# RWKV-7 recurrence on one core: value pieces in halves, three copies moved to ScalarE, and a new hand-written order of the four interleaved programs

## What is computed

```python
def _wkv_step(S, inp):
    r_t, w_t, k_t, v_t, a_t, b_t = inp
    Sa = jnp.einsum('bhvk,bhk->bhv', S, a_t)
    S = S * w_t[:, :, None, :] + Sa[..., None] * b_t[:, :, None, :] + v_t[..., None] * k_t[:, :, None, :]
    y = jnp.einsum('bhvk,bhk->bhv', S, r_t)
    return S, y
...
    k = xk @ w_k
    v = xv @ w_v
    a = jax.nn.sigmoid(a0 + (xa @ a1) @ a2)
    kk = kk / jnp.maximum(jnp.sqrt(jnp.sum(kk * kk, axis=-1, keepdims=True)), 1e-12)
    k = k * (1 + (a - 1) * k_a)
...
    S_last, ys = lax.scan(_wkv_step, wkv_prev.astype(f32), xs)
    y = ((y - ym) * lax.rsqrt(yv + GN_EPS)).reshape(B, T, D) * gn_g.astype(f32) + gn_b.astype(f32)
    y = (y + bonus.reshape(B, T, D)).astype(x.dtype)
    out = (y * g) @ w_o
```

## Time and profile before

| | us |
|---|---|
| median of 3 runs | 2713.64 |
| lowest, highest | 2710.94, 2715.29 |
| the profiled execution, own time | 2709.54 |
| its span | 2708.0 |

### The profile page before, as it was taken

One profiled execution on the slowest core, in us unless ns is written; L12 is line 12 of the kernel. 1 busy time (PEld: TensorE's weight loads), 2 busy tenths in 40 slices (PEclk: granted clock), 3 DMA queues, 4 the chain that ended last, 5 costly groups with the idle time before them and its releaser, 6 DMA issues.

```text
span 2708.0 us, 56286 instructions
## 1 busy us (share of the span) xinstructions
PE 2584.9 (95%) x23289; PEld 2475.8 (91%) x23289; DVE 1583.1 (58%) x2411; ACT 1127.6 (42%) x1580; POOL 142.2 (5%) x211
## 2 busy tenths in 40 slices
PE   7979999999999899999999999969999999999997
PEld 6977878888788799999999999958999999999997
DVE  6877878888856644444444444586444444444446
ACT  4564555555433533333333333445333333333334
POOL 1000111111101100000000000100000000000000
PEclk9999999999999999999999999979999999999999
DMA  7532323222335666556665556624565566565563
GB/s 227 155 84 69 83 83 82 75 79 81 97 99 165 166 168 168 160 144 167 185 169 166 161 144 167 180 73 116 163 170 160 145 166 186 165 170 161 144 166 94
DMA packets 707051, 379.30 MB, mean 140 GB/s; under 512 B 16023, under 2 KB 699191, under 8 KB 706711
## 3 DMA queue, kind: packets, MB, share of 16 engines
q1 hardware_dynamic: 701040, 363.42, 48.0%
q0 software_dynamic: 5792, 13.34, 1.9%
q10 hardware_dynamic: 70, 0.39, 0.1%
HBM read 367.28 MB, written 10.62 MB: 140 GB/s over the span
## 4 chain that ended last, share of the span: by engine, by line
PE 80%; DVE 13%; ACT 4%; issue 2%; DMA 0%; DVEq 0%; SPq 0%; ACTq 0%; POOL 0%
PE PS L708 24%; PE PS L709 24%; PE PS L710 24%; PE PS L855 2%; DVE WL L1647 2%; ACT WH L1225 1%; DVE PL L1749 1%; DVE TM L1791 1%; DVE TM L1655 1%; DVE ML L1662 1%; PE PS L887 1%; ACT PH L1318 1%; DVE XL L1887 1%; PE PS L725 1%; PE PS L929 0%
## 5 line engine op out<-in xcount | busy, mean ns | idle before, releaser
L1647 DVE TENSOR_TENSOR WL<-RAW,WH 128x2048 fp32r<-128x2048 f32 (+1 forms) x325 | 658.6, 2027 | 764.4 <-ACT WH L1225 764.4
L708 PE MATMUL PS<-MH,WH 128*128 128x288 f32 (+1 forms) x3152 | 933.3, 296 | 25.0 <-DVE ML L2046 11.8
L709 PE MATMUL PS<-ML,WH 128*128 128x288 f32 (+1 forms) x3152 | 934.7, 297 | 0.0
L710 PE MATMUL PS<-MH,WL 128*128 128x288 f32 (+1 forms) x3152 | 933.7, 296 | 0.0
L1225 ACT ACTIVATE WH<-RAW 128x2048 fp32r<-128x2048 f32 (+1 forms) x325 | 553.3, 1702 | 822.8 <-PE PS L710 808.4
L708 PEld LDWEIGHTS PS<-MH,WH 128*128 128x128 f32 (+1 forms) x3152 | 596.3, 189 | 31.1 <-issue 20.1
L709 PEld LDWEIGHTS PS<-ML,WH 128*128 128x128 f32 (+1 forms) x3152 | 596.6, 189 | 0.2
L710 PEld LDWEIGHTS PS<-MH,WL 128*128 128x128 f32 (+1 forms) x3152 | 595.9, 189 | 0.0
L709 PE MATMUL PS<-HL,WH 128*128 128x288 f32 x1408 | 415.3, 295 | 0.0
L710 PE MATMUL PS<-HH,WL 128*128 128x288 f32 x1408 | 415.0, 295 | 0.0
L708 PE MATMUL PS<-HH,WH 128*128 128x288 f32 x1408 | 413.4, 294 | 0.0
(11 more groups left out here) (304 smaller groups left out, 2718.7 us busy)
## 6 DMA issues: line engine op xcount, KB each, us to landing
RAW<-in_ffn_w_in SPq DMA_DIRECT2D x176, 1024.0 KB, 5.7
RAW<-in_ffn_w_down SPq DMA_DIRECT2D x128, 704.0 KB, 4.8
RAW<-in_rw_wr SPq DMA_DIRECT2D x16, 1024.0 KB, 6.1
PR<-in_rw_wk SPq DMA_DIRECT2D x64, 256.0 KB, 3.1
PR<-in_rw_wv SPq DMA_DIRECT2D x64, 256.0 KB, 3.1
PR<-in_rw_wo SPq DMA_DIRECT2D x64, 256.0 KB, 3.3
S0N<-in_state_wkv POOLq DMA_DIRECT2D x64, 64.0 KB, 2.4
out<-SOS POOLq DMA_DIRECT2D x64, 64.0 KB, 2.7
```

The lines of the kernel that those rows point to most:

```text
L708: pe.matmul(out, wh, xh, start=first, stop=False)
L709: pe.matmul(out, wh, xl, start=False, stop=False)
L710: return pe.matmul(out, wl, xh, start=False, stop=last)
L1647: dve.tensor_tensor(WL[0:rows, j % 2, 0:n], RAW[0:rows, j, 0:n], WH[0:rows, j % 2, 0:n].bitcast(F32), ALU.subtract).then_inc(lo_ready, 1)
```

## The change

It does the following.
- TensorE: the last three v pieces (6 to 8) are taken in halves of six matmuls, each a stretch of its own (`half`); the first low-rank product follows k's last piece, and the second stands with v piece 5. DENSE has 12 stretches instead of 11.
- The y products with the states, two for each state, move behind u3, and the states keep four places. The transposes of the final state, step "fin", get a step apart from "y".
- ScalarE takes three kinds of copy from VectorE: the decayed state SPD (three to a chunk), the result y into R, and YS.
- VectorE: the normalisation is closed with two fused operations where there were three; the reciprocal of the key norm is made in halves; RKP comes later; the masks RB and KR stand behind the transpose, and `norm("rest")` behind x0.
- New strings of letters.

```diff
-        ORDER = {"pe": "FDBDFBFDBFDBFDDFBDBFBDBFBFBDBFBDBDF", "dve": "FBFDFDBDBDFBDFFBDBFBBDFBDBDFBDFDBBF",
-                 "act": "FBFBDDFDDFDBBFDBDFBFBDBDFBFBFDDFBBB"}
+        ORDER = {"pe": "FDBDFBFDFBDFFBDFBDFBDFBDFBDFBDBBDBD", "dve": "FBFDFDBDBDFBFFFBDFBDFBDFBDDFBDFBBBDBD",
+                 "act": "FBDFBDFDBFBDDFFBFBFDBFBDDFBDFBDBBBDD"}
...
                     for j in range(4):
                         columns(D0, j, 4 * j, MH[1], ML[1])
+                        if j == 3:
+                            ready(other.dact, "v", ago)
+                            arrived(4)
+                            z.dpe.done(low_rank(D1, 0), "w")
                         yield
...
-                    for j in range(5, 9):
-                        columns(D1, j, 4 * (j - 5), MH[0], ML[0])
+                    columns(D1, 5, 0, MH[0], ML[0])
+                    yield
+                    for j in range(6, 9):
+                        half(D1, j, 4 * (j - 5), 0, MH[0], ML[0])
+                        yield
+                        half(D1, j, 4 * (j - 5), 1, MH[0], ML[0])
...
+                    if c == 3:
+
+                        for d in range(1, 4):
+                            for h in range(2):
+                                pe.matmul(PA[hr[h], col(d // 2, d % 2)], z.ST[hr[h], d, :],
...
-                    slots = {0: 2, 1: 3, 2: 4, 3: 5, 4: 6, 6: 7, 7: 8, 8: 9, 9: 10}
+                    slots = {0: 2, 1: 3, 2: 4, 3: 5, 4: 6, 5: 7, 7: 8, 9: 9, 11: 10}
...
+                    await_step(z.dve, f"st{c - 1}")
+                    z.act.done(act.activation(z.SPD[:, :], z.ST[:, c, :], ACT.Copy,
+                                              scale=z.PC[:, (c + 1) * CH - 1:(c + 1) * CH]), f"spd{c}")
...
+                await_step(z.dve, "yout")
+                z.act.done(act.activation(one(R, p)[:, 0:SEQ], PA[:, 0:SEQ], ACT.Copy), "yr")
...
-                        linked(dve.tensor_tensor(y, y, z.YT, ALU.mult), "norm")
-                        linked(dve.tensor_scalar(y, y, par("gn_g", c), par("gn_b", c), ALU.mult, ALU.add), "scale")
-                        z.ndve.done(dve.tensor_tensor(y, y, z.BON, ALU.add), "done")
+                        linked(dve.scalar_tensor_tensor(out=y, in0=y, scalar=par("gn_g", c), in1=z.YT, op0=ALU.mult,
+                                                        op1=ALU.mult), "norm")
...
+                            z.ddve.done(dve.reciprocal(z.YT[:, 0:T // 2], z.YT[:, 0:T // 2]), "inv0")
...
+                            z.ddve.done(dve.reciprocal(z.YT[:, T // 2:T], z.YT[:, T // 2:T]), "inv1")
...
-                z.dve.done(dve.tensor_scalar(one(R, p)[:, 0:SEQ], PA[:, 0:256], 1.0, None, ALU.mult), "yr")
```

More of the change, by code:

```diff
@@ L345, in build @@
         later = [f"{n}{c}" for c in range(1, 4) for n in ("u", "s")]
-        PE_STEPS = (["s0", "tok", "prod"] + levels + ["q", "s0c"] + later + ["y"])
-        DVE_STEPS = (["cs", "csx", "kt", "kt2", "bfa", "rkp", "feats", "sm", "tit", "ti", "turn", "masks"]
+        PE_STEPS = (["s0", "tok", "prod"] + levels + ["q", "s0c"] + later + ["y", "fin"])
+        DVE_STEPS = (["cs", "csx", "kt", "kt2", "bfa", "feats", "rkp", "sm", "tit", "ti", "turn", "masks"]
                      + ["x0", "t0", "turn0", "x1", "t1", "turn1", "x2", "t2", "utc", "turn2", "uvx"]
                      + ["x3", "t3", "snw", "turn3", "snw2", "x4", "t4", "bonv", "st0"]
[L350 to L356, removed]
+                     + [f"{n}{c}" for c in range(1, 4) for n in ("u", "st")]
+                     + ["yout"])
+        ACT_STEPS = ["decays", "s0t", "tok", "wr", "qt", "ys", "sos", "mv", "q", "spd1", "spd2", "spd3", "yr", "sop"]
+        DENSE_STEPS = dict(pe=["w", "kn"], act=["k", "kk", "sq", "sg", "a", "root", "v"], dve=["inv0", "inv1", "unit"])
+        NORM_STEPS = dict(pe=["mean", "var"], dve=["cen", "rstd", "norm", "done"], act=["sq", "var", "sd"])
         class Steps:
@@ L812, in columns, with half @@
                         ins.then_inc(pc_used, 1)
+                    def half(bank, j, k0, part, xh, xl):
+                        if part == 0:
+                            arrived(j)
+                        slot = j % 3
+                        for k in (2 * part, 2 * part + 1):
+                            ins = three(bank[:, 0:T], PH[slot][:, k * P:(k + 1) * P], PL[slot][:, k * P:(k + 1) * P],
+                                        xh[:, k0 + k, :], xl[:, k0 + k, :], k0 + k == 0, k0 + k == KC - 1)
+                        if part == 1:
+                            ins.then_inc(pc_used, 1)
                     def low_rank(bank, n):
@@ L1828, in pair @@
                     z.dve.done(dve.tensor_tensor(z.BF[:, :], z.KK, z.A, ALU.mult), "bfa")
-                    link(dve.scalar_tensor_tensor(out=z.RKP, in0=one(R, p), scalar=par("r_k", p), in1=z.K,
-                                                  op0=ALU.mult, op1=ALU.mult), "rkp")
                     yield
                     await_step(z.act, "decays")
+                    await_step(z.dve, "bfa")
                     dve.scalar_tensor_tensor(out=z.AR[:, 0, :], in0=z.KK, scalar=-1.0, in1=z.CSX[:, :], op0=ALU.mult,
@@ L1839, in pair @@
                     yield
+                    z.dve.done(dve.scalar_tensor_tensor(out=z.RKP, in0=one(R, p), scalar=par("r_k", p), in1=z.K,
+                                                        op0=ALU.mult, op1=ALU.mult), "rkp")
                     yield
@@ L1889, in pair @@
                     yield
+                    if lv == 0:
+                        norm("rest")
+                        yield
                     await_step(z.pe, f"t{lv}")
@@ L1926, in pair @@
                     end = z.PC[:, (c + 1) * CH - 1:(c + 1) * CH]
-                    await_step(z.dve, f"st{c - 1}")
-                    z.dve.done(dve.tensor_scalar(z.SPD[:, :], z.ST[:, r, :], end, None, ALU.mult), f"spd{c}")
                     await_step(z.pe, f"u{c}")
@@ L1934, in pair @@
                     await_step(z.pe, f"s{c}")
[L1935 to L1936 removed]
+                    await_step(z.act, f"spd{c}")
+                    z.dve.done(dve.scalar_tensor_tensor(out=z.ST[:, (c + 1) % 4, :], in0=PC[:, 384:384 + HN],
                                                         scalar=end, in1=z.SPD[:, :], op0=ALU.mult, op1=ALU.add),
```

79 lines of the change are left out of this document (40 added, 39 removed).

## The result

| | before | changed kernel |
|---|---|---|
| median, us | 2714.3 | 2800.1 |
| lowest to highest | 2710.9 to 2715.3 | 2795.9 to 2806.4 |
| profiled execution, span | 2708.0 | 2799.5 |

The changed kernel takes 1.032 times as long, 95% interval 1.0298 to 1.0342. The forecast was 2783.6 us, in a range of 2742 to 2822, and slower.

A forecast was written before the change was run, and what follows sets the result against it. TensorE was taken to set the pace: waits 5.5, stretches +0.5, gains −1.2 make +4.8 us a weave, +67 over fourteen, +3 for the first; profiled 2709.5 to 2779.5, plus 4.1 gives 2783.6 us, range 2742 to 2822.

The forecast's parts named there:

- What bounds the kernel: In the recurrence TensorE sets the pace; hiding all its waits brings about 1.2 us a weave, 17 us over fourteen.
- The four waits: New TensorE waits in each weave: 1.8 us at x0 (t4 0.3 late), 0.9 at t1, 0.8 at t2, 1.3 at u3.
- The 0.1 at v's piece 6: TensorE between the waits at x0 and t1, beside VectorE's long row of 6.1 us: nothing to 0.3 us, taken as 0.1.
- the 0.3 at s3: TensorE waits 0.3 us at s3 for u3's update, with only the moved y products ahead of it.
- Price of more stretches: TensorE's dense blocks go from nine to eleven; 0.25 us for each extra one, +0.5 us a weave.
- What goes: Earlier TensorE waits, such as that for the last state, vanish or are counted among the new ones: −1.2 us a weave.
- the copies: With other edits, copies moved to ScalarE relieve VectorE of some 1.4 us a weave, but buy nothing where the order waits.
- The sum: Waits, stretches and gains give +4.8 us a weave, +67 over fourteen, first weave +3, the end 0: 2783.6 us.
- Rival C: The clock falls to 1.2 GHz once in each weave because of the waits: +24 us, so 2807; 20 in 100.
- A: The added waits are hidden after all, if p5 passes MV on ScalarE: −0.7 us a weave, 2704 us; 10 in 100.
- B: Only x0's wait and half of the others come, covers being short by half a us: +43, 2757 us; 22 in 100.
- The load of a table: ScalarE, before the root ahead of t2: counted 1.28 us; with the skill's drain of 1.38 us, whole some 19 us longer.

The follow-up runs named there:

- c6_half: c5_p7_early with v's piece 7 alone taken in halves, six of its matmuls ahead of t1: 2705.4 us, ratio 0.9971 to before.
- a4_inv1: Changed kernel with p5 ahead of MV, p7 and p8 ahead of MVS, root ahead of QT, reciprocal's second half behind the last state: 2719.9 us, one run.
- c5_p7_early: Code edits without halves, TensorE's order of before, VectorE and ScalarE reordered, p7's low part ahead of state 1: 2703.1 us, ratio 0.9962 to before.
- b1_p5_late: Kernel before with t4 ahead of k's last piece on TensorE, and p5, k and p6 behind MV on ScalarE: 2756.4 us, ratio 1.0161.
- f2_fill: Changed kernel with extra matmuls put into TensorE's waits at x0, t1, t2 and u3: 2809.0 us, ratio 1.0360 to before.

## Why the prediction held, point by point

**What bounds the kernel.** Right. TensorE paced the weaves, had about 1 us of waits in each to give back, and the order across engines decided.

**The four waits.** Forecast 0.3 and 1.8 us at t4 and x0, 0.9 at t1, 0.8 at t2, 1.3 at u3; measured 0.27 and 1.82, 0.82, 0.71, 1.22. The causes at x0, t1 and t2 were shown by moving that one step back: each wait in turn left the list. u3's more than halved in two steps; t4's 0.27 was not tried. The 0.1 at v's piece 6 and the 0.3 at s3 are too short for the rows of waits. The weave's idle time is 40.40 − 35.34 = 5.06 us, so 0.22 are left for both: 0.10 before piece 6, as forecast, and 0.12 before s3 instead of 0.3.

**Price of more stretches.** This term was too small. The forecast was 0.25 us for a stretch, 0.5 in all. c6_half shows 0.35, so 0.7 for two. The whole change brought 35.34 − 34.48 = 0.86 us of work into a weave, and a4_inv1, with the changed kernel's eleven dense blocks, has 35.28. The way into a block, which I allowed 0.1 for, is the part I had no row for; what the other 0.15 are no run shows.

That the weave still came out as forecast (40.4 against 40.3) is partly luck, since three errors cancel: waits of 5.1 us instead of 5.5, work of 0.86 instead of 0.5, and 1.05 us of idle time to take off instead of 1.2. The 1.2 was a mean over 300 to 700 us, where two long weaves raise it, and I took it from 35.5, which is the weave without them.

**What goes, and the copies.** The wait for the last state is gone from the list, as forecast. That the copies buy nothing where the order waits fits the rows, in which VectorE waits 1.4 to 2.3 us for ScalarE at three places of a weave; no run takes the copies alone out of the changed kernel. c5_p7_early shows what they are worth with another order: −0.5 us a weave against before, together with its better places for masks and states. TensorE's work in a weave is the same there (34.42 for 34.48 us), so what went is idle time.

**The sum.** The forecast was +70 us on the profiled execution, fourteen weaves and 3 us for the first; its span grew by 91.5. The first weave gave 1.5 us and not 3. The next thirteen gave 77.5 (542.0 for 464.5) where 13 x 4.8 is 62.4: the mechanism's size was right, 40.4 us where the clock held, but 13 x 40.4 is only 525.2, so 17 us of them are what the half-clock stretches cost, which I had left out. The last one, before the output product, with PEclk at a half for 10 us, grew by 9.1 and not 4.8. After the weaves 3 us came where I said 0. They are in c5_p7_early too (1983.2 us behind the weaves, before 1980.0), which has no halves, and not in b1_p5_late (1979.5), so they come with the code edits or with the strings of `TAIL`; no run parts the two. These make the 21.5 us too many. The median of before lay 4 us above its profiled execution, and that of the changed kernel lies 1 below, which leaves the 16.5 between 2783.6 and 2800.1.

**Rival C was no rival but an addition.** I gave it as once in every weave, 24 us, and on the whole unlikely, since before kept the full clock through waits of up to 1.8 us. It came in nine of thirteen weaves, and 2800.1 us is nearer to C's 2807 than to my 2783.6: the waits were right, and most of what the sum lacked is the clock. f2_fill settles that it follows the waits. Why equal waits bring it in one weave and not in the next I cannot say.

**Rivals A and B.** A asked that p5 pass MV; ScalarE's rows show MV and then p5, 0.28 us apart. The Trainium skill's "PSUM — Partial Sum Buffer", section "Engine vs sequencer instructions", says that the queues of these engines are strictly in order, and the trace agrees. B asked for covers short by half a us at three places; they were out by 0.1 at t1, t2 and u3.

**The load of a table.** The row holds again: the load starts at 468.82, takes 1.28 us, and the root starts at 470.11. A drain behind it, which the Trainium skill's "ScalarE: Activation LUTs" puts at about 1380 ns in "What ACT_TABLE_LOAD costs", is not to be seen, and the wait at t2, 0.71 us, has no room for it.
